# Splitting q, k and every gate tile, and scanning partly in PSUM, in a hybrid state-space and attention block

## The reference, cut to what matters

```python
h = layer_norm(x, ln_in_g, ln_in_b)
proj = h @ w_in[l]
u, q, k, v, q_idx, k_idx, w_idx, gate_pre = jnp.split(proj, split_points, axis=-1)
y_ssm = s5_branch(u, ...)             # complex scan over positions, 2048 states, then GELU and GLU
y_att = dsa_branch(q, k, v, q_idx, k_idx, w_idx) @ w_attn_proj[l]   # index scores, top 128 keys, softmax
g_ssm, g_att = jnp.split(jax.nn.sigmoid(gate_pre + b_gate[l]), N_BRANCHES, axis=-1)
mix = (g_ssm * y_ssm + g_att * y_att) @ w_o[l]
h = layer_norm(DEEPNORM_ALPHA * h + mix, ln1_g[l], ln1_b[l])
h = layer_norm(DEEPNORM_ALPHA * h + moe_ffn(h, ...), ln2_g[l], ln2_b[l])   # top 4 of 32 experts
```

## Time and profile before

| | |
|---|---|
| median of 3 runs | 1703.63 us |
| the profiled execution | 1704.47 us |
| its span in the profile | 1702.7 us |
| TensorE, VectorE, ScalarE, GpSimd busy | 1643.0, 1502.7, 1074.3, 473.0 us |
| state loop | from 39 to 219 us |
| gate tiles and index scores | from 214 to 320 us |
| attention, GLU | from 320 to 409 us |

### The profile page before, as it was taken

The page is one execution under the profiler, slowest core; times in us unless marked ns, Lnnn a source line. Parts: engine busy times, 40 slices in busy tenths (PEclk is TensorE's granted clock), DMA queues, the critical chain, the costliest instruction groups (busy, mean ns, idle before and its releaser), DMA issues.

```text
span 1702.7 us, 22448 instructions
## 1 busy us (share of the span) xinstructions
PE 1643.0 (96%) x7233; PEld 1104.8 (65%) x7233; DVE 1502.7 (88%) x1684; ACT 1074.3 (63%) x1046; POOL 473.0 (28%) x295
## 2 busy tenths in 40 slices
PE   5999999999988999999999999999999999999996
PEld 3333457765775777777777777777777777777763
DVE  6999989666679899999999999999999999999995
ACT  5444234344455777777777777777777777777771
POOL 4533144672442121222212122122221212212210
PEclk9899999999988999999999999999999999999998
DMA  5111121313158899999999999999999999999973
GB/s 178 49 53 50 50 87 63 124 50 124 35 187 317 335 362 362 369 376 369 369 363 378 363 369 365 366 374 356 372 363 366 372 370 365 364 370 374 372 279 108
DMA packets 91902, 464.78 MB, mean 273 GB/s; under 512 B 21289, under 2 KB 21405, under 8 KB 42616
## 3 DMA queue, kind: packets, MB, share of 16 engines
q1 hardware_dynamic: 80240, 441.67, 67.9%
q0 software_dynamic: 9776, 18.41, 4.4%
q10 hardware_dynamic: 1848, 4.24, 0.7%
HBM read 454.15 MB, written 18.53 MB: 278 GB/s over the span
## 4 chain that ended last, share of the span: by engine, by line
PE 84%; DVE 12%; issue 2%; ACT 1%; DMA 1%; POOL 0%; ACTq 0%; DVEq 0%; POOLq 0%
PE ps L1859 20%; PE ps L1861 20%; PE ps L1860 20%; PE ps L1845 3%; PE ps L1867 2%; PE ps L1540 2%; PE ps L1554 2%; PE ps L1642 1%; PE ps L1643 1%; PE ps L1644 1%; PE ps L1634 1%; DVE w_lo L1266 1%; PE ps L1548 1%; DVE scr L1134 1%; DVE scr L1135 1%
## 5 line engine op out<-in xcount | busy, mean ns | idle before, releaser
L1266 DVE TENSOR_TENSOR w_lo<-raw,w_hi 128x2048 fp32r<-128x2048 f32 x384 | 872.6, 2289 | 73.9 <-ACT w_hi L907 73.8
L907 ACT ACTIVATE w_hi<-raw 128x2048 fp32r<-128x2048 f32 x384 | 736.9, 1919 | 241.1 <-PE ps L1861 239.8
L1859 PE MATMUL ps<-w_hi,x_hi 128*96 128x512 f32 x1024 | 415.0, 405 | 0.0
L1861 PE MATMUL ps<-w_lo,x_hi 128*96 128x512 f32 x1024 | 402.8, 393 | 0.0
L1860 PE MATMUL ps<-w_hi,x_lo 128*96 128x512 f32 x1024 | 402.3, 393 | 0.0
L1859 PEld LDWEIGHTS ps<-w_hi,x_hi 128*96 128x96 f32 x1024 | 168.3, 164 | 67.2 <-issue 2.0
L1861 PEld LDWEIGHTS ps<-w_lo,x_hi 128*96 128x96 f32 x1024 | 165.6, 162 | 71.3
L1859 PE MATMUL ps<-w_hi,a_hi 128*96 128x512 f32 x512 | 203.9, 398 | 5.7 <-DVE a_lo L1377 5.7
L1860 PEld LDWEIGHTS ps<-w_hi,x_lo 128*96 128x96 f32 x1024 | 166.1, 162 | 63.8
L640 POOL DMA_INDIRECT gate_now<-gate_rows,row_now x32 | 79.9, 2498 | 455.2 <-DVE tok_out L1407 440.0
L1860 PE MATMUL ps<-w_hi,a_lo 128*96 128x512 f32 x512 | 201.5, 394 | 0.0
(11 more groups left out here) (339 smaller groups left out, 2155.8 us busy)
## 6 DMA issues: line engine op xcount, KB each, us to landing
raw<-in_w_up SPq DMA_DIRECT2D x256, 1024.0 KB, 6.8
raw<-in_w_down SPq DMA_DIRECT2D x128, 1024.0 KB, 9.8
ring<-in_w_in SPq DMA_DIRECT2D x9, 2048.0 KB, 7.7
ring<-in_w_glu SPq DMA_DIRECT2D x4, 1024.0 KB, 6.2
ring<-in_w_o SPq DMA_DIRECT2D x2, 2048.0 KB, 13.4
h<-in_x SPq DMA_DIRECT2D x4, 512.0 KB, 5.0
ring<-in_w_attn_proj SPq DMA_DIRECT2D x1, 2048.0 KB, 8.0
h_rows<-h ACTq DMA_DIRECT2D x4, 512.0 KB
```

The costliest lines, as they stand in the source:

```text
L907: s.activation(hi_of(c)[:, :], raw_of(c), ACT.Copy).then_inc(s_hi, 1)
L1266: d.tensor_tensor(lo_of(c)[:, :], raw_of(c), hi_of(c)[:, :], ALU.subtract).then_inc(s_lo, 1)
L1859: mm(o, xh, hi_of(c)[:, col], start=start, stop=False)
L1861: return mm(o, xh, lo_of(c)[:, col], start=False, stop=stop)
```

## The change

- All q, k and gate tiles are split; u, qi, ki, wi and v stay native. The order of tiles is now u, qi, ki, v0, wi, v1 to v3, q0 to q3, g0 to g3, k0 to k3, g4 to g15. The first 22 are in the state loop as before, the last 16 behind it.
- The parts of the stream are made in the loop: upper parts in the place of `h` itself, lower parts in place of the transposed stream `hT` that the native tiles read, a quarter of the tokens at a time, each once the v tile that reads that quarter is done. The last quarter is first copied to `h_tail`, and v3 reads that. The upper parts of the weights have two buffers; the second lies where `h_tail` is, so it is filled once v3 is done.
- The phase lies in the half of ring slot 3 that k will take, as v is now made earlier.
- As `h` is overwritten, `x` is loaded a second time after the last gate tile, and GpSimd normalises it again (one more instruction for each of four tiles).
- In `s5` the two cosine products are written into the PSUM banks they read, the real part's sum goes to PSUM bank 4, and its scan reads and writes that bank. The pair of blocks is released after six instructions (the sums with them) instead of four. The outputs of `ymm` 0 to 2 share bank 5.
- The ReLU outputs get other buffers, the first eight one each.

```diff
-        phase, whole = v, [ring[:, 4, 2624:3136], ring[:, 4, 3136:3648]]
+        phase, whole = ring[:, 3, 2048:4096].rearrange("p (k t) -> p k t", k=4), [ring[:, 4, 2624:3136], ring[:, 4, 3136:3648]]
...
-        h_hi = [over(f"h_hi{r}", [P, 4, SEQ], F32R, at_scr, 2048 * b) for r, b in enumerate((12, 4))]
-        h_lo = [over("h_lo0", [P, 4, SEQ], F32R, at_gb), over("h_lo1", [P, 4, SEQ], F32R, at_scr, 2048 * 8)]
-        gate_hi = [over("gate_hi0", [P, KD, P], F32R, at_ring, 4 * 2 * CHUNK), over("gate_hi1", [P, KD, P], F32R, at_bias3)]
+        h_hi = over("h_hi", [P, KD, SEQ], F32R, at_h)
+        h_lo = over("h_lo", [P, KD, SEQ], F32R, at_ring, 4 * 2 * CHUNK)
+        h_tail = over("h_tail", [P, KD, P], F32, at_route)
+        part_hi = [over("part_hi0", [P, KD, P], F32R, at_bias3), over("part_hi1", [P, KD, P], F32R, at_route)]
...
-        FRONT = [("u", C_U), ("qi", C_QI), ("q", C_Q), ("k", C_K), ("v", C_V)]
-        FRONT += [("g", C_G + 512 * i) for i in range(4)]
+        FRONT = [("u", C_U), ("qi", C_QI), ("v", C_V), ("q", C_Q), ("g", C_G), ("k", C_K)]
+        FRONT += [("g", C_G + 512 * i) for i in range(1, 4)]
...
-        for kind, lo, hi in (("u", 0, 4), ("qi", 0, 4), ("ki", 0, 1), ("q", 0, 1), ("wi", 0, 1), ("q", 1, 4), ("k", 0, 4),
-                             ("v", 0, 4), ("g", 0, 16)):
+        for kind, lo, hi in (("u", 0, 4), ("qi", 0, 4), ("ki", 0, 1), ("v", 0, 1), ("wi", 0, 1), ("v", 1, 4), ("q", 0, 4),
+                             ("g", 0, 4), ("k", 0, 4), ("g", 4, 16)):
...
-                    sp.wait_ge(s_tile, first_tile["gg"])
+                    sp.wait_ge(s_tile, SPLIT1)
+                    for t in range(TT):
+                        sp.dma_start(h[:, t, :], x_v[:, t, :]).then_inc(s_x[t], 16)
...
+            def stream_lower(i):
+                x = slice(P * i, P * i + P)
+                if i == 0:
+                    pool.wait_ge(s_hhi, KD)
+                if i < TT - 1:
+                    pool.wait_ge(s_tile, v_tiles[i] + 1)
+                else:
+                    pool.wait_ge(s_tail, 1)
+                g.tensor_tensor(h_lo[:, :, x], hT[:, :, x], h_hi[:, :, x], ALU.subtract).then_inc(s_hlo, 1)
+                pool.wait_ge(s_hlo, i + 1)
+
+            def weights_lower(n):
+                pool.wait_ge(s_phi, n - SPLIT0 + 1)
+                g.tensor_tensor(part_lower(n), part_weights(n), part_upper(n)[:, :, :], ALU.subtract).then_inc(s_plo, 1)
+                pool.wait_ge(s_plo, n - SPLIT0 + 1)
+
...
+                if j >= 11:
+                    if j < 15:
+                        stream_lower(j - 11)
+                    if j >= 12:
+                        weights_lower(SPLIT0 + j - 12)
...
+            pool.wait_ge(s_causal, 1)
+            weights_lower(SPLIT0 + 4)
...
-            pool.wait_ge(s_lnT, KD)
+            pool.wait_ge(s_xhat, TT)
             for t in range(TT):
+                pool.wait_ge(s_x[t], 32)
+                step(g.tensor_scalar(h[:, t, :], h[:, t, :], mvx[:, t, 0:1], rsx[:, t, 1:2], ALU.subtract, ALU.mult))
...
+            def stream_upper(k):
+                s.activation(h_hi[:, k, :], hT[:, k, :], ACT.Copy).then_inc(s_hhi, 1)
+
+            def weights_upper(n):
+                if n >= SPLIT1:
+                    return
+                if (n - SPLIT0) % 4 == 0:
+                    wait_chunk(act, chunk_of(n))
+                if n == SPLIT0 + 1:
+                    act.wait_ge(s_tile, SPLIT0)
+                elif n >= SPLIT0 + 2:
+                    act.wait_ge(s_tile, n - 1)
+                s.activation(part_upper(n)[:, :, :], part_weights(n), ACT.Copy).then_inc(s_phi, 1)
+
+            def take_next(n):
+                if n >= SPLIT0:
+                    act.wait_ge(s_tile, n + 1)
+                    weights_upper(n + 2)
+                take(n)
...
-            TAKEN_BY = [1, 2, 3, 4, 5, 7, 8, 10, 11, 13, 14, 15, 16, 18, 19, 20]
+            TAKEN_BY = [0, 1, 2, 3, 5, 6, 7, 8, 10, 11, 12, 14, 15, 16, 18, 20]
...
+                if 3 <= j < 7:
+                    stream_upper(2 * j - 6)
+                    stream_upper(2 * j - 5)
+                if j == 8:
+                    s.activation(h_tail[:, :, :], hT[:, :, 3 * P:], ACT.Copy).then_inc(s_tail, 1)
                 while n <= TAKEN_BY[j]:
-                    take(n)
+                    take_next(n)
                     n += 1
-            act.wait_ge(s_stfree, 3)
-            stream_upper(0, 4)
-            while tiles[n][0] != "g":
-                take(n)
-                n += 1
+                    if n == SPLIT0 - 2:
+                        weights_upper(SPLIT0)
+                    if n == SPLIT0:
+                        weights_upper(SPLIT0 + 1)
+            take_next(n)
...
-                step(d.tensor_tensor(m[:, 0, :], br[:, :], c, ALU.mult))
+                re = ps[4]
                 step(d.tensor_tensor(m[:, 1, :], bi[:, :], sn, ALU.mult))
-                step(d.tensor_tensor(m[:, 2, :], bi[:, :], c, ALU.mult))
-                d.tensor_tensor(m[:, 3, :], br[:, :], sn, ALU.mult).then_inc(s_bufree, 1)
+                step(d.tensor_tensor(m[:, 3, :], br[:, :], sn, ALU.mult))
+                step(d.tensor_tensor(br[:, :], br[:, :], c, ALU.mult))
+                step(d.tensor_tensor(bi[:, :], bi[:, :], c, ALU.mult))
+                step(d.tensor_tensor(re[:, :], br[:, :], m[:, 1, :], ALU.add))
+                d.tensor_tensor(m[:, 2, :], bi[:, :], m[:, 3, :], ALU.subtract).then_inc(s_bufree, 1)
                 dve.wait_ge(s_bufree, j + 1)
-                step(d.tensor_tensor(m[:, 0, :], m[:, 0, :], m[:, 1, :], ALU.add))
-                step(d.tensor_tensor(m[:, 2, :], m[:, 2, :], m[:, 3, :], ALU.subtract))
                 decay = spw[:, 2, j:j + 1].to_broadcast([P, SEQ])
-                step(d.tensor_tensor_scan(m[:, 1, :], decay, m[:, 0, :], 0.0, ALU.mult, ALU.add))
+                step(d.tensor_tensor_scan(re[:, :], decay, re[:, :], 0.0, ALU.mult, ALU.add))
                 step(d.tensor_tensor_scan(m[:, 3, :], decay, m[:, 2, :], 0.0, ALU.mult, ALU.add))
                 if j >= 5:
                     dve.wait_ge(s_stfree, (j - 5) // 4 + 1)
                 w = w_st[j % 5]
-                step(d.tensor_tensor(w[:, 0, :], m[:, 1, :], c, ALU.mult))
+                step(d.tensor_tensor(w[:, 0, :], re[:, :], c, ALU.mult))
                 step(d.tensor_tensor(w[:, 1, :], m[:, 3, :], sn, ALU.mult))
-                step(d.tensor_tensor(w[:, 2, :], m[:, 1, :], sn, ALU.mult))
+                step(d.tensor_tensor(w[:, 2, :], re[:, :], sn, ALU.mult))
...
+                elif kind in ("q", "k", "g"):
+                    if n == SPLIT0:
+                        pe.wait_ge(s_hlo, TT)
+                    pe.wait_ge(s_plo, n - SPLIT0 + 1)
+                    for k in range(KD):
+                        mm(o[:, :], part_upper(n)[:, k, :], h_hi[:, k, :], start=k == 0, stop=False)
+                        mm(o[:, :], part_upper(n)[:, k, :], h_lo[:, k, :], start=False, stop=False)
+                        ins = mm(o[:, :], part_lower(n)[:, k, :], h_hi[:, k, :], start=False, stop=k == KD - 1)
...
-            order = [(0, 3), (1, 4), ("small", 1), (2, 1), ("wi", 1), (2, 3), (3, 4), (4, 4)]
-            flat = [c for c, cnt in order for i in range(cnt)]
-            bu_at = {1: 1, 4: 2, 7: 3, 10: 4, 13: 5, 15: 6, 18: 7}
-            y_at = {6: 0, 12: 1, 17: 2}
+            flat = [0, 0, 0, 1, 1, 1, 1, "small", 2, "wi", 2, 2, 2, 3, 3, 3, 3, 4, 4, 4, 4]
+            bu_at = {1: 1, 4: 2, 6: 3, 8: 4, 11: 5, 14: 6, 17: 7}
+            y_at = {5: 0, 10: 1, 15: 2}
...
-            def gate_tile(n):
...
+            def key_or_gate(i):
+
+                if i % 4 == 0:
+                    arrive(5 + i // 4)
+                tile(n + i, 5 + i // 4)
```

More of the change, by code:

```diff
@@ L48 @@
 POOL_ROUNDS = 3
-NATIVE = 3
-RELUS = 8
 MORE = range(1, -(-SEQ // BLK))
@@ L1616, in _ @@
                     pe.wait_ge(s_small, 16)
-                elif c != "wi" and c != (flat[i - 1] if i else 0):
+                elif c != "wi" and c not in flat[:i]:
                     arrive(c)
```

170 lines of the change are left out of this document (65 added, 105 removed).

## The result

The changed kernel takes 1710.07 us, median of 6 executions (1707.15 to 1713.14), the kernel before 1704.41, median of 6 (1702.93 to 1709.06). The ratio is 1.0026, 95% interval 1.0013 to 1.0038, which is 4.4 us with an interval from 2.2 to 6.5 (the medians lie 5.7 us apart). The loss is small and yet real: no gain, and on the other side of no change than the forecast. The time lies inside the range given (1692 to 1711) and outside the forecast case's own range (1698 to 1705). The profiled execution of the changed kernel took 1707.15 us (span 1705.4); it is the fastest of the six.

The account below looks back on a forecast made before the run. VectorE paces until 171 us, then TensorE. Cheaper tiles (16.5 us) and about 9 us lighter VectorE work, after stall and clock, leave 3.1, less 0.5 for GpSimd: 2.6 us faster, 1701.0 us, range 1692 to 1711.

Parts of the forecast that it names:

- the forecast case: The main outcome of the whole forecast, 2.6 us faster, with its own range 1698 to 1705 and chance 0.49.
- VectorE paces up to v3: State loop: TensorE's `bu` 5 needs block 9's sixth instruction at 140.4, both engines level there, v3 over at 149.7.
- Block 9 was forecast at 136.0: VectorE in the state loop: lighter blocks 0 to 8 let block 9 start at 136.0 instead of 145.5.
- the rival by which writing PSUM costs: VectorE's block: four instructions writing PSUM get slower; chance 0.12 small (1701 to 1710), 0.13 large (over 1712).
- The stall: Between v3 and q0: TensorE idles 10.4 us for the stream's fourth quarter on GpSimd, so q0 starts at 160.1.
- the half microsecond for a hindered GpSimd: Chain before q0: 0.5 us taken off the 3.1 us gain because GpSimd is hindered there.
- `bu` 6 was forecast at 175.4: State loop, behind q1 on TensorE: block 12, possible at about 170, has to wait until 177.3.
- Behind the stall I took 4.2 us: TensorE from q0: after the idle time the clock falls to half for 8.5 us, losing 4.2 us of work.
- the forecast's 1.1: VectorE, blocks 0 to 8: 1.1 us added for a wait for `bu` 2 and for GpSimd's new work.
- TensorE gets to g3's end at about 216, later than block 15's release at 213.5, so it doesn't wait: End of the state loop: blocks behind 12 start at 187.5, 199 and 209, so TensorE isn't held up again.
- The forecast's 1701.9: Forecast time of the profiled execution: 1704.5 less 2.6 us; against the median the forecast was 1701.0.
- The rival without the stall (1691): Between v3 and q0: q0 follows v3 at once, gate tiles end at 307.6, 13 us earlier; chance 0.09.

Follow-up runs that it names:

- e5: Changed kernel without the second load of x, h cleared by memsets instead; total 1884.5 us, not comparable because its experts get other work.
- e13: Changed kernel with fourth quarter early, h_tail moved, score work one tile later, and GpSimd's q0 to k0 weight subtractions replaced by ScalarE zeros: 1695.1 us.
- e14: The kernel before, unchanged, profiled a second time; last gate tile over at 320.1 us.
- e8: Changed kernel with only h_tail moved, so the upper part of q1's weights needn't wait for v3: 1696.7 us, ratio 0.9950.
- e9: e8 with every tile of the score part moved one place up on TensorE, so score work comes one tile later: 1693.7 us, ratio 0.9937.

## Why the prediction was wrong, step by step

**Right.** VectorE paces up to v3. Block 9 was forecast at 136.0 and starts at 136.03, but that agreement is luck: the loop starts 1.6 us later than in the kernel before (the early fall of the clock), and blocks 0 to 8 take 95.1 us instead of 96.7. v3 is over at 149.5 (149.7). Operands in PSUM cost nothing (0.70, 1.23), so the rival by which writing PSUM costs fell. By the rule of the Trainium skill's page "VectorE: DVE Perf Modes" (section on the TRN2 errata) an instruction from PSUM would take 0.065 us longer, as an estimate; the trace of the changed kernel doesn't show it (at 220.49 L1171 reads PSUM, at 221.22 L1172 reads SBUF alone, both 0.69). The stall: q0 forecast at 160.1, in the trace

```profile
161.05 0.77 PE L1594 MATMUL ps<-h_hi,part_hi 128*128 128x512 f32 x1 [11.57 <-POOL h_lo L549]
```

The stall was forecast at 10.4 us; the half microsecond for a hindered GpSimd was 1.2, its phase instructions taking 2.06, 1.59 and 0.93 beside VectorE. `bu` 6 was forecast at 175.4, starts at 173.7, and block 12 waits 8.00 us for it. The second load of x is hidden (e5).

**The clock, mis-sized twice.** Behind the stall I took 4.2 us, from the earlier trace rows. q0, q1 took 12.6 us to `bu` 6 against 11.1 at full clock: 1.5 us. The slow clock had begun at about 154 while TensorE stood idle, and most of it ran out there:

```profile
154.00:156.00 2.00, 0.00 (x0) 0.00 (x0) 1.93 (x3) 0.00 (x0) 1.92 (x2) 0.50 1.05 399
158.00:160.00 2.00, 0.00 (x0) 0.00 (x0) 1.93 (x3) 0.00 (x0) 1.92 (x2) 0.50 0.00 0
```

On the other hand I priced no fall behind the short waits. There are four: behind `bu` 1 (1.48 us of waiting, low from 58 to 62), behind `bu` 4 (1.15, v1 takes 8.83 instead of 7.06), behind `dots` (3.27), and before the GLU (1.84). The first two lie where VectorE paces: behind the first, VectorE waits 0.77 us for `bu` 2, which the forecast's 1.1 covers, and behind the second `bu` 5 still waits for VectorE. The other two cost 1.7 and 1.65 us. With the 1.5 at q0 the clock costs 4.85 us in all; that this is near the 4.2 forecast is luck, as most of it stands at other places:

```profile
218.00:220.00 2.00, 1.92 (x9) 1.28 (x10) 1.97 (x2) 0.00 (x0) 0.46 (x1) 0.63 1.05 410
220.00:222.00 2.00, 2.00 (x6) 1.53 (x6) 1.90 (x4) 0.00 (x0) 0.00 (x0) 0.51 0.90 335
```

**The step that failed: "TensorE gets to g3's end at about 216, later than block 15's release at 213.5, so it doesn't wait".** It got there at 214.8, and the release came at 217.9, so it waited 3.27 us. I let blocks 12 to 15 follow each other in 10.2, 11.5 and 10 us, 31.7 in all, 1.6 over three undisturbed ones and `y_out` (30.1); they took 11.4, 14.0 and 12.5, 37.9 in all, 7.8 over. GpSimd's nine weight subtractions for q0 to k0 now stand in the loop ahead of that release, seven of them behind q0's start, and I had charged the block only for the work before block 9. Block 14, changed kernel, with GpSimd's two subtractions beside it:

```profile
206.71 1.85 DVE L1167 TENSOR_TENSOR_SCAN scr<-spw,scr 128x512 f32<-128x512 f32 x1
...
210.76 2.79 DVE L1174 TENSOR_TENSOR gb<-scr 128x512 f32<-128x512 f32 x1
```
```profile
205.07 2.40 POOL L554 TENSOR_TENSOR wg_lo<-ring,part_hi 128x1024 fp32r<-128x1024 f32 x1 [5.24 <-ACT part_hi L805]
210.61 2.40 POOL L554 TENSOR_TENSOR wg_lo<-ring,part_hi 128x1024 fp32r<-128x1024 f32 x1 [3.14 <-ACT part_hi L805]
```

The product at 210.76 ends at 213.55, 0.54 us after the subtraction beside it, and the scan at 208.56, 1.09 after its one; alone they take 0.69 and 1.22. e13 shows the cause by taking the subtractions away. The forecast also had `far` done near 309; it is done at 315.6, still ahead of the end of the gate tiles, so that costs nothing.

**The account.** The forecast's 1701.9 stands for a last gate tile over at 318.1, which is 317.6 and the 0.5 for GpSimd. In the trace its last matmul ends at 321.85 (GpSimd follows at 322.0), 3.75 later. `dots` start 2.1 us later than the forecast's 216.0 (VectorE's blocks), and from there it takes 103.8 us instead of 101.6, of which 1.7 is clock; the 0.5 comes off, as it lies ahead of the `dots`. Behind the tile come 1.65 of clock. 1701.9 + 3.75 + 1.65 = 1707.3; the profiled execution took 1707.15. To the median of 1710.07 it is 2.9 us more. The profiles put what varies behind attention, equally for both kernels, and don't explain it further. At the end of attention the changed kernel is 1.1 us late where neither profile has the early fall of the clock (e5, 409.5, against 408.4), and 2.9 to 3.5 where both have it (410.7 and 411.2 against 407.7 in e14). The rest of the loss of 4.4 us stays open.

The rival without the stall (1691) was wrong for this kernel, since the stall is there. Its walk is close to what e8 does with the stall nearly gone: block 15's release about 206, where `dots` wait for it until 205.93, and the last gate tile at 307.6, where it is over at 309.9. Its sum left out the falls of the clock behind `dots` and before the GLU, 1.7 us each in e8; the time is 1696.7. With another place for the score work e9 took 1693.7.
